# A planned instruction order: the second tile's block goes ahead of the first mixer for 80 steps, gathers may be paced by landings, late routing keeps its normal place

## What is computed

```python
def chunk(args):                       # 128 tokens at a time
    xi, ei, gi = args                  # ei: 128 experts for each token (8 heads x 16)
    hid = jax.nn.gelu(jnp.einsum("td,tkd->tk", xi, u_tab[ei]))
    return jnp.einsum("tk,tkd->td", gi * hid, v_tab[ei])
```

## Time and profile before

| | |
|---|---|
| median of three executions | 2239.04 us |
| the profiled execution | 2236.08 us |
| its span, first to last instruction | 2234.3 us |
| busy: PE, DVE, ACT, POOL | 1671.9, 1438.2, 807.7, 588.9 us (75, 64, 36, 26%) |
| weight loads on PE | 985.1 us (44%) |
| gathers: bytes, share of the 16 DMA engines | 536.90 MB, 59.2% |
| weights and the rest by SyncE | 236.04 MB, 26.7% |
| all DMA | 774.25 MB, mean 347 GB/s |
| mean granted TensorE clock | 0.875 of full speed |

### The profile page before, as it was taken

The page is one execution under the profiler, slowest core; times in us unless marked ns, Lnnn a source line. Parts: engine busy times, 40 slices in busy tenths (PEclk is TensorE's granted clock), DMA queues, the critical chain, the costliest instruction groups (busy, mean ns, idle before and its releaser), DMA issues.

```text
span 2234.3 us, 20472 instructions
## 1 busy us (share of the span) xinstructions
PE 1671.9 (75%) x6628; PEld 985.1 (44%) x6628; DVE 1438.2 (64%) x3501; ACT 807.7 (36%) x2055; POOL 588.9 (26%) x516
## 2 busy tenths in 40 slices
PE   7988988848766776875467887665888766677776
PEld 3448774724246625454124535422554532222222
DVE  2323344198687767767985866778778578854444
ACT  2322213135345622631334442233445233343333
POOL 0000000001433331242342343343423333343331
PEclk9979999968877887987798898888999888799999
DMA  9556864634999999889899989999999979899997
GB/s 358 211 192 244 301 228 168 264 146 184 413 419 419 419 420 400 323 338 375 337 367 420 383 350 419 397 376 357 406 417 368 419 306 383 338 421 420 420 420 315
DMA packets 108523, 774.25 MB, mean 347 GB/s; under 512 B 12160, under 2 KB 12416, under 8 KB 16256
## 3 DMA queue, kind: packets, MB, share of 16 engines
q0 software_dynamic: 73728, 536.90, 59.2%
q1 hardware_dynamic: 34688, 236.04, 26.7%
HBM read 771.85 MB, written 1.05 MB: 346 GB/s over the span
## 4 chain that ended last, share of the span: by engine, by line
DMA 39%; PE 36%; DVE 15%; ACT 4%; issue 4%; POOL 2%; SPq 0%; DVEq 0%; POOLq 0%; ACTq 0%
DMA arena<-in_peer_dram,eidx 13%; DMA kv<-in_peer_dram,eidx 10%; PE psum L728 8%; PE psum L1061 8%; DMA ring<-in_peer_dram,eidx 8%; DMA ring<-in_slabs_dram 7%; PE psum L714 7%; PE psum L918 6%; DVE x L1932 2%; PE psum L936 2%; DVE arena L1922 1%; DVE kv L1922 1%; DVE smi L1735 1%; PE psum L893 1%; DVE smi L1746 1%
## 5 line engine op out<-in xcount | busy, mean ns | idle before, releaser
L2071 POOL DMA_INDIRECT arena<-in_peer_dram,eidx x254 | 293.9, 1157 | 1085.6 <-DVE eidx L1793 458.7
L1061 PE MATMUL psum<-arena,diag 128*128 128x512 f32 x692 | 366.7, 664 | 167.3 <-ACT diag L1384 155.7
L1922 DVE CUSTOM_DVE_ANT_0 arena<-arena,osb 128x1024 f32<-128x1024 f32 x254 | 308.9, 1223 | 164.1 <-DMA arena<-in_peer_dram,eidx 163.3
L1374 ACT ACTIVATE wexp<-hid 128x1 f32<-128x1 f32 x512 | 103.1, 201 | 784.3 <-DVE hid L1922 783.2
L1061 PEld LDWEIGHTS psum<-arena,diag 128*128 128x128 f32 x692 | 136.0, 210 | 371.1 <-ACT diag L1384 228.2
L714 PE MATMUL psum<-ring,hT 128*128 128x512 f32 x560 | 260.2, 619 | 12.3 <-DMA ring<-in_slabs_dram 9.5
L1061 PE MATMUL psum<-kv,diag 128*128 128x512 f32 x344 | 180.8, 653 | 56.6 <-ACT diag L1384 28.7
L2071 POOL DMA_INDIRECT ring<-in_peer_dram,eidx x129 | 154.3, 1196 | 259.8 <-PE psum L1061 133.9
L728 PE MATMUL psum<-hT,ring 128*128 128x128 f32 x1536 | 191.0, 289 | 34.1 <-DMA ring<-in_slabs_dram 26.2
L1922 DVE CUSTOM_DVE_ANT_0 ring<-ring,osb 128x1024 f32<-128x1024 f32 x129 | 157.8, 1224 | 89.8 <-DMA ring<-in_peer_dram,eidx 89.5
L2071 POOL DMA_INDIRECT kv<-in_peer_dram,eidx x129 | 140.5, 1089 | 271.9 <-PE psum L1061 121.8
(11 more groups left out here) (315 smaller groups left out, 1911.1 us busy)
## 6 DMA issues: line engine op xcount, KB each, us to landing
ring<-in_slabs_dram SPq DMA_DIRECT2D x206, 1024.0 KB, 8.4
ring<-in_slabs_dram SPq DMA_DIRECT2D x8, 768.0 KB, 6.9
ring<-in_slabs_dram SPq DMA_DIRECT2D x8, 512.0 KB, 5.0
arena<-in_peer_dram,eidx POOLq DMA_INDIRECT x254, 12.8
kv<-in_peer_dram,eidx POOLq DMA_INDIRECT x129, 12.2
ring<-in_peer_dram,eidx POOLq DMA_INDIRECT x129, 14.3
kk<-in_keys_dram SPq DMA_DIRECT2D x2, 1024.0 KB, 10.9
rowg<-in_rows_dram SPq DMA_DIRECT2D x3, 512.0 KB, 21.3
```

The costliest lines, as they stand in the source:

```text
L1061: ins = pe.matmul(bank(b), diags_of(n), pair(slot_of[n])[:, 1024 + 512 * h:1536 + 512 * h], start=(k == 0), stop=(k == 127))
L1374: act.activation(wn, hid[:, 128 * t + k:128 * t + k + 1], ACT.Gelu_apprx_tanh).then_inc(*up("gelu", n))
L1922: v.tensor_tensor_reduce(out=row, in0=row, in1=row_y[t], scale=1.0, scalar=0.0, op0=ALU.mult, op1=ALU.add, accum_out=hid[:, c:c + 1]).then ...
L2071: pool.indirect_dma_start(pair(i), None, tables, bass.IndirectOffsetOnAxis(ap=eidx[:, 128 * t + k:128 * t + k + 1], axis=0)).then_inc(sig. ...
```

## The change

It has five parts. (1) While the tensor program has done fewer than `T_HEAD` = 80 steps of B1, steps of M00, R00 and C00 have wish 1.3, so B1 (1.04) goes first. (2) `T_KEEP` goes from 3 to 4 and `T_LATE` from 2.0 to 0.0. (3) Only Q00 keeps the special wishes; Q01, Q10 and Q11 have the normal one, and `late()` counts Q01 for the second expert tile and Q10 for the third. (4) While tile 0 is gathered and B1 has tensor steps left, or later while the chain is late, gather n also waits for the landing of gather n - `T_FLIGHT` = n - 8. (5) `measure` notes a slab as used up in the step with its last signal. `T_SHRINK` = 0 and `T_END` = 0 leave the ring's shrinking and the end of the pacing as the code would be without them.

```diff
--- before.py
+++ after.py
@@ -30,7 +30,7 @@
 
 
 
-T_MB, T_SEEN, T_ISSUE, T_DOT, T_WEIGHT, T_DIAG, T_TENSOR, T_VECTOR, T_TABLE, T_HOP, T_KEEP, T_LEAN, T_AHEAD, T_LATE, T_PACE = 2.5, 2.0, 1.15, 1.35, 0.55, 0.42, 2.0, 1.35, 1.28, 0.12, 3, -2.0, 14, 2.0, 3.0
+T_MB, T_SEEN, T_ISSUE, T_DOT, T_WEIGHT, T_DIAG, T_TENSOR, T_VECTOR, T_TABLE, T_HOP, T_KEEP, T_LEAN, T_AHEAD, T_LATE, T_PACE, T_SHRINK, T_FLIGHT, T_END, T_HEAD = 2.5, 2.0, 1.15, 1.35, 0.55, 0.42, 2.0, 1.35, 1.28, 0.12, 4, -2.0, 14, 0.0, 3.0, 0, 8, 0, 80
 ENGINES = ("PE", "DVE", "ACT")
 
 K_ID, K_MC, K_MD, K_CD, K_ONE, K_IO, K_IF, K_SEL, K_END = 0, 128, 640, 1152, 1664, 1792, 1808, 1840, 1850
@@ -429,7 +429,7 @@
 
 
         plan, gathers, takes, consumed = {e: [] for e in ENGINES}, [], [], {}
-        ways = {}
+        ways, paced = {}, {}
 
         def measure(stage, meter):
 
@@ -439,8 +439,10 @@
                 while r != "end":
                     meter.way, known = [], len(consumed)
                     r = next(stage[s], "end")
-                    meter.way += [("used", key) for key in list(consumed.values())[known:]]
                     found[s].append(meter.way)
+                    for key in list(consumed.values())[known:]:
+                        last = [way for way in found[s] if ("signal", key) in way][-1]
+                        last.append(("used", key))
             consumed.clear()
             return found
 
@@ -518,15 +520,17 @@
                 tile = counts["dot"] // 128
                 if tile > 2:
                     return False
-                left = sum(left_of[e, s][at_step[e, s]] for s in (("B1", "M01"), ("M01", "M10"), ("M10", "M11"))[tile] for e in ENGINES)
+                left = sum(left_of[e, s][at_step[e, s]] for s in (("B1", "M01"), ("M01", "Q01", "M10"), ("M10", "Q10", "M11"))[tile] for e in ENGINES)
                 return (128 * tile + 128 - counts["dot"]) * T_PACE < left
 
             def wish(s, i):
 
-                if s[0] == "Q":
+                if s == "Q00":
                     tile = ORDER.index((int(s[1]), int(s[2])))
                     routed = sum(1 for hh in range(4) if ("routed", *ORDER[tile], hh) in seen)
                     return 0.9 if len(gathers) > 128 * tile + 32 * routed - T_AHEAD else 1.5
+                if s in ("M00", "R00", "C00") and at_step["PE", "B1"] < T_HEAD:
+                    return 1.3
                 return 1 + 0.01 * i
 
             def choices(e, now):
@@ -632,16 +636,21 @@
                 routed = ready([("routed", *ORDER[n // 128], n % 128 // 32)])
                 if routed is None:
                     return False
-                if n == 0:
+                if n == T_SHRINK:
                     load_slabs()
                     two[0] = len(loaded)
                     slots[6] = slots[7] = ("ring", 0)
-                if ("ring", 0) not in seen and used.get(two[0] - 3) in seen:
+                if n >= T_SHRINK and ("ring", 0) not in seen and used.get(two[0] - 3) in seen:
                     seen["ring", 0] = seen[used[two[0] - 3]]
                 free = [(seen[key], i) for i, key in slots.items() if key in seen]
                 if not free:
                     return False
                 when, i = min(free)
+                if (n < 128 and at_step["PE", "B1"] < len(ways["PE"]["B1"]) - T_END or n >= 128 and late()) and n >= T_FLIGHT:
+                    if ("landed", n - T_FLIGHT) not in seen:
+                        return False
+                    when = max(when, seen["landed", n - T_FLIGHT])
+                    paced[n] = n - T_FLIGHT
                 slots[i] = ("taken",)
                 clock["POOL"] = max(clock["POOL"], when, routed) + T_ISSUE
                 pairs[n] = i
@@ -2068,6 +2077,8 @@
                 else:
                     w.wait_ge(*at(*consumed.get(two[0] - 3, ("ffn_down", 1, 5))))
                 w.wait_ge(*at("routed", l, t, k // 32))
+                if n in paced:
+                    w.wait_ge(sig.sem("row%d" % slot_of[paced[n]]), landed_at[paced[n]])
                 pool.indirect_dma_start(pair(i), None, tables, bass.IndirectOffsetOnAxis(ap=eidx[:, 128 * t + k:128 * t + k + 1], axis=0)
                                         ).then_inc(sig.sem("row%d" % i), 16)
                 held[i] = n
```

## The result

The changed kernel takes 2145.99 us (median of 4, 2143.18 to 2147.31) against 2240.24 us for the kernel before on the same chip: a ratio of 0.958, 95% interval 0.956 to 0.960. The forecast was 2205 us with a range of 2168 to 2256. The direction was right, the size was not: 94 us were gained and not 31.

The account below looks back on a forecast made before the run. The time was taken as first gather, bytes left at 420 GB/s and DMA idleness behind it. Terms of -46 + 25 + 46 + 6 gave 31 us gained, from 2236.1 to 2205 us, range 2168 to 2256.

Parts of the forecast that it names:

- The frame: Whole kernel: time is first gather, plus bytes left at 420 GB/s, plus DMA idleness behind the first gather (202 us).
- The head start: B1's first 80 steps ahead of M00: 46 us lost, 25 gained by earlier weight loads, 46 by less idleness.
- The delay X: How much later the first gather comes because B1's work goes ahead: 46 us, bounds 36 and 95.
- Break-even: Rival: X near 75, or the hole only halved, 2229 to 2243 us; chance 0.13 together with the inert case.
- The delay eats it: The slower rival: B1's attention keeps its own waits ahead of M00, X is 95, 2260 us; chance 0.21.
- the hole: DMA idleness of 64 us right behind the first gather, 458 to 558 us: 46 us gained, 18 left.
- Buffer threshold and bias: T_KEEP 4 and T_LATE 0: 6 us gained from idleness between 893 and 1059 us, bounds -10 and +28.
- More than the sum: Rival: later mixers run ahead of the gathers, idleness from 1812 to 1955 us closes, 2171 us; chance 0.20.
- the late rule and the routing wishes: Normal wishes for Q01, Q10, Q11 and counting Q01 as work left: 0 us, wishes bounded 5 either way.
- pacing: Gather n waiting for the landing of n - 8: always met already, 0 us, at most 36 us in all.
- The moved marks: Slabs noted as used one step sooner in the planner: 0 us, bounds 10 either way.
- The signs: Among them: first gather about 505 us, B1's last down slab near 800, second tile's first gather near 1030, later spacing unchanged.

Follow-up runs that it names:

- 10: The kernel before with the moved used marks and T_KEEP 4: 2168.96 us, ratio 0.970.
- 11: The kernel before with the moved used marks, T_HEAD 80 and T_KEEP 4, nothing else: 2144.2 us, ratio 0.958.
- run 1: The changed kernel without the head start (T_HEAD 0): 2174.4 us, ratio 0.973 to the kernel before.
- C: The changed kernel itself, with all five parts, against the kernel before: 2145.99 us, ratio 0.958.
- 6: The kernel before with the moved used marks alone: 2243.72 us, ratio 1.003.
- 9: The kernel before with the moved used marks and T_HEAD 80, thresholds as before: 2208.22 us, ratio 0.988.
- run 2: The changed kernel with T_KEEP 3 again: 2210.05 us, ratio 0.989 to the kernel before.
- 3: The changed kernel with the old wishes for Q01, Q10 and Q11 and the old late rule: 2145.32 us, ratio 0.958.
- 4: The changed kernel without the added waits for landing n - 8: 2145.68 us, ratio 0.960.

## Why the prediction was wrong in size

**The frame held.** First gather, bytes and idleness give 90 us for a span that fell by 89.8.

**The head start was right in its sum, wrong in its terms.** Forecast -46 + 25 + 46 = 25 us; runs give 25 (experiments 10 and 11), 28 (1 and C) and 36 (6 and 9). The delay X of the first gather was 75 us, not 46, where the rival "Break-even" stood and just below the 77 from which the slower rival decided. TensorE was busy 406.9 of the 458 us before the first gather and is busy 484.5 of 534: it does 78 us more work, where I had 56, and stands as long as before, 50 us and not 51, where I had let the work fill 10. The trace says why: the forecast let B1's first 80 steps go ahead, some 58 us of TensorE, but B1 does not stop there. From 416 us TensorE hardly idles, and what M00 leaves free in its own waits goes to B1's other four gate slabs and its branches, where I had counted three slabs in all, and these run in front of M00's steps that become ready meanwhile. VectorE's 44 empty microseconds did not help, for they lie beside the query weights, which moved with everything else. Against it, the hole closed by 58 us and not 46 (5 us of idleness are left, I had left 18), and 32 us of bytes went ahead and not 25. These add up to -76 + 32 + 58 = 14 us; the rest of the first tile gives 9 more between run 1 and C (16 us of idleness to 7). That the sum came near 25 is luck: three errors of 7 to 30 us and a part that was not priced nearly cancelled.

**The step that failed is "Buffer threshold and bias": 6 us, where T_KEEP measured 64** (41 alone, 75 on top of the marks). I priced the idle time only up to 1059 us, and left the 92 us behind it as they were. They became 43, and with T_KEEP back at 3 they are 89 (run 2): 46 of the 64 us. A move of more than 20 us there was the forecast's own sign of being wrong. Two readings led there. First, in the rival "More than the sum" I took 15.8 us of waiting before 1818.8 us for late routing. The row names TensorE's L1061 as the releaser, so it was a wait for a buffer; the fourth tile's routing at 1822 us had 21 older gathers still ahead of it. Had I counted gathers at the routing times, the sign would have been plain: in the later tiles the chain was ahead and the rows behind, so priority moved from the chain to the rows, up to where they meet, gains. Second, I asked what one buffer more or less costs in steps and not what it does to the rows in flight. With T_KEEP 3 peer work goes first only when five of eight buffers are full, which leaves three for rows under way; with 4 it is four. The gathers under way, by the estimate of experiment 2 (3.3 to 3.4, then 4.1), agree; that nothing else in the order has a part in it is not shown. What the runs show is the lag of 23 rows with 3 (21 in B), 1 with 4, 0 with 5, and times of 2210, 2146 and 2188 us.

**T_LATE** was nothing of the 6 us. 73 accumulations on VectorE between 492 and 847 us did become 19 between 534 and 770 us, but not because of the bias: with 2.0 again both the count of accumulations (105) and the time are the same. In the planner's account it is because C's chain is hardly late.

**Right:** the late rule and the routing wishes inert (3), pacing free (4), though by the planner's own account 47 gathers are paced and not 75 to 120. **The moved marks** cost or gain little alone (1.003), as forecast, but I missed two things: the head start isn't planned without them, and T_KEEP 4 gains 26 us more with them (2169 against 2195).

**The signs.** Four of the forecast's signs came: eight gathers within 12 us, then no wait of the gather queue over 15 us, B1's attention over before 430 us (at 416), and over 300 GB/s (398) in the 50 us behind the first gather. The first gather came at 534.5 us, far from 505 and just inside the 535 that would have said wrong. B1's last down slab is done at 768 us and the second tile's first gather is at 1011, 32 and 19 us sooner than forecast. VectorE stayed empty ahead of the key scores, and the spacing of the later tiles changed.

**The rivals.** "More than the sum" came nearest with 2171 us, but for another reason than it gave: the later mixers did not run further ahead of the gathers. The fourth tile's routing was 37 us sooner, but the second tile's was 54 us sooner already. And there are still 27 us of idleness from 1745 to 1938 us, where that rival wanted it closed. Two of the rivals' sums were off. The 8 us for half of the idleness left before 1059 us should by the forecast's own terms (18 + 4 + 22) be 22, so 2157 us. "The delay eats it" leaves out the 6 us of T_KEEP, which its bound of 77 counts; with them it is 2254 us. POOL's timeline of the changed kernel shows the like of the earlier trace rows still there, again a wait for a buffer:

```profile
1777.11 0.93 POOL L2082 DMA_INDIRECT arena<-in_peer_dram,eidx  x1 [14.40 <-PE psum L1070]
```

VectorE's timeline shows what held the buffers:

```profile
1759.82 0.50 DVE L1740 MAX8 sm<-psum 128x8 f32<-128x128 f32 x2 [9.80 <-PE psum L1036]
...
1770.78 1.22 DVE L1931 CUSTOM_DVE_ANT_0 arena<-arena,osb 128x1024 f32<-128x1024 f32 x1
```

It stands 9.8 us for M11's key scores and then works on the routing of the first pair of heads for 11 us; only from 1770.8 us on does it take dots again, one right behind the other. So the rows stand behind the last steps of M11. In the kernel before it was the same: VectorE routed from 1800 to 1812 us and took dots again at 1812.5. The routing was not late for the gathers, but its work held the buffers. Whether that can be closed was not tried.

**The rule.** I had set 420 GB/s against the 358 that the Trainium skill's page DMA: Bandwidth & Descriptors gives under "Where 436 GB/s comes from", as a stack's 716 GB/s divided between two cores; this kernel runs on one. The changed kernel moves 411 GB/s on average over 734 us, gathers and weights mixed, so the measurement decides again against that figure. Of the 134 us of idleness that went, 76 lay behind the hole, where that figure would leave next to none.

## What to carry to other kernels

When a chain that prepares work and a stream that delivers data share engines, count how far the stream is behind (or ahead) at each point where the chain hands over; that count says which of them to favour. Here one unit of a threshold was worth more than a large reordering, and one unit further cost 42 us again. When a stage is let ahead "for N steps", price also what it will fill in with once it is ahead. And look twice at who ended a wait before calling it late work: the releaser's line tells a missing buffer from a missing index, and what the releaser's own inputs waited for tells who held the buffer.

## What was not expected of the hardware

That the DMA engines hold 410 GB/s and more with rows of 8 KB gathered by index and weights mixed, for hundreds of microseconds, while all three compute engines work: 409 GB/s over 399 us and 414 GB/s over 161 us. In the kernel before the best stretch of that kind was 415 GB/s over 335 us, and the others had 344 to 399. With T_KEEP 3 in the otherwise same kernel the 409 are 383 GB/s over 417 us (run 2), so in that tile the difference was the order of work.
